# Loading, splitting and multiplying the first weight tile of an encoder kernel in pieces, and x by halves of its columns

## The reference

```python
def _rmsnorm(x, g):
    xf = x.astype(jnp.float32)
    y = xf * lax.rsqrt(jnp.mean(xf * xf, axis=-1, keepdims=True) + RMS_EPS)
    return (y * g.astype(jnp.float32)).astype(x.dtype)

def _pool_mixer(h, w_in, w_group, scale, w_out):
    b, s, _ = h.shape
    u = (h @ w_in).reshape(b, s, N_POOL_GROUPS, POOL_GROUP)
    ...
    mixed = pooled - u
    y = jnp.einsum('bsgc,gcd->bsgd', mixed, w_group).reshape(b, s, -1) * scale
    return y @ w_out

def reference(x, ...):
    for i in range(DEPTH):
        hn = _rmsnorm(x, norm_mix[i])
        ...
        x = x + y
        hn = _rmsnorm(x, norm_ffn[i])
        ...
        x = x + y
    return _rmsnorm(x, norm_final)
```

## Time and profile before

| | |
|---|---|
| median of 3 runs | 1656.31 us (1655.06 to 1656.72) |
| the profiled execution | 1656.18 us, span 1654.4 us |
| mean granted TensorE clock | 0.995 of full speed |
| TensorE busy (matmuls) | 1622.1 us, 98% |
| VectorE busy | 1205.2 us, 73% |
| ScalarE busy | 1015.3 us, 61% |
| HBM read | 455.86 MB, 276 GB/s over the span |

### The profile page before, as it was taken

The page is one execution under the profiler, slowest core; times in us unless marked ns, Lnnn a source line. Parts: engine busy times, 40 slices in busy tenths (PEclk is TensorE's granted clock), DMA queues, the critical chain, the costliest instruction groups (busy, mean ns, idle before and its releaser), DMA issues.

```text
span 1654.4 us, 22146 instructions
## 1 busy us (share of the span) xinstructions
PE 1622.1 (98%) x8139; PEld 1339.8 (81%) x8139; DVE 1205.2 (73%) x969; ACT 1015.3 (61%) x837; POOL 86.6 (5%) x107
## 2 busy tenths in 40 slices
PE   8999999999899999999999999999999999999996
PEld 6888888899699877888888888888888888888885
DVE  4554454454654568888888887887888887887886
ACT  5444443433633466767767777777777777777774
POOL 0000000050331220000000000000000000000000
PEclk9999999999999999999999999999999999999998
DMA  9555555476166417999999999999999999998992
GB/s 364 164 181 181 194 182 178 153 248 195 68 202 205 153 52 244 357 367 319 363 360 320 360 361 324 356 361 322 357 362 321 358 362 321 362 358 325 358 361 87
DMA packets 234392, 457.74 MB, mean 277 GB/s; under 512 B 9008, under 2 KB 15152, under 8 KB 234336
## 3 DMA queue, kind: packets, MB, share of 16 engines
q1 hardware_dynamic: 231216, 454.06, 78.9%
q10 hardware_dynamic: 3120, 2.91, 0.6%
HBM read 455.86 MB, written 1.08 MB: 276 GB/s over the span
## 4 chain that ended last, share of the span: by engine, by line
PE 95%; DVE 2%; ACT 1%; issue 1%; DMA 0%; SPq 0%; ACTq 0%; DVEq 0%
PE bY L273 9%; PE bY L275 9%; PE bY L274 9%; PE bG L273 8%; PE bG L274 8%; PE bG L275 8%; PE bU L275 8%; PE bU L274 8%; PE bU L273 8%; PE bS L274 3%; PE bS L275 3%; PE bS L273 3%; PE bT L493 2%; DVE logit L1155 1%; PE bX L275 1%
## 5 line engine op out<-in xcount | busy, mean ns | idle before, releaser
L263 DVE TENSOR_TENSOR wlo<-raw,whi 128x2048 fp32r<-128x2048 f32 x427 | 979.9, 2295 | 364.7 <-ACT whi L257 362.3
L257 ACT ACTIVATE whi<-raw 128x2048 fp32r<-128x2048 f32 x427 | 818.6, 1917 | 471.1 <-PE bY L275 182.2
L273 PE MATMUL bU<-whi,eTh 128*128 128x512 f32 x448 | 181.4, 405 | 0.0
L273 PE MATMUL bG<-whi,eTh 128*128 128x512 f32 x448 | 178.9, 399 | 1.1 <-ACT eTl L772 1.1
L273 PE MATMUL bY<-whi,hTh 128*128 128x512 f32 x448 | 179.0, 400 | 0.0
L274 PE MATMUL bG<-whi,eTl 128*128 128x512 f32 x448 | 178.7, 399 | 0.0
L275 PE MATMUL bG<-wlo,eTh 128*128 128x512 f32 x448 | 178.5, 398 | 0.0
L274 PE MATMUL bU<-whi,eTl 128*128 128x512 f32 x448 | 177.6, 396 | 0.0
L274 PE MATMUL bY<-whi,hTl 128*128 128x512 f32 x448 | 177.5, 396 | 0.0
L275 PE MATMUL bU<-wlo,eTh 128*128 128x512 f32 x448 | 177.5, 396 | 0.0
L275 PE MATMUL bY<-wlo,hTh 128*128 128x512 f32 x448 | 177.4, 396 | 0.0
(11 more groups left out here) (384 smaller groups left out, 2390.4 us busy)
## 6 DMA issues: line engine op xcount, KB each, us to landing
raw<-in_m_w_gate_up_dram SPq DMA_DIRECT2D x224, 1024.0 KB, 5.1
raw<-in_m_w_down_dram SPq DMA_DIRECT2D x112, 1024.0 KB, 5.0
raw<-in_b_w_in_dram SPq DMA_DIRECT2D x36, 1024.0 KB, 5.0
raw<-in_f_w_gate_up_dram SPq DMA_DIRECT2D x28, 1024.0 KB, 5.1
raw<-in_f_w_down_dram SPq DMA_DIRECT2D x14, 1024.0 KB, 4.9
raw<-in_a_w_in_dram SPq DMA_DIRECT2D x4, 1024.0 KB, 11.1
raw<-in_a_w_out_dram SPq DMA_DIRECT2D x4, 1024.0 KB, 14.0
biasrev<-toeplitz SPq DMA_DIRECT2D x32, 128.0 KB, 4.6
```

What stands on the lines that cost most here:

```text
L257: nc.scalar.activation(whi[:, t % CUT], raw[:, t % RAW], ACT.Copy).then_inc(hi_done, 1)
L263: nc.vector.tensor_tensor(wlo[:, t % CUT], raw[:, t % RAW], whi[:, t % CUT].bitcast(F32), ALU.subtract).then_inc(lo_done, 1)
L273: pe.matmul(dst, a[0], b[0], start=start, stop=False)
```

## The change

x is loaded in eight pieces instead of four, each 64 tokens by 512 columns, and has one semaphore for each half of the columns (`load_x`). The first halves go first: two from SP, two from ACT, between its loads of the identity and of `gainT`. SP then loads tile 0 in four pieces (one block of 128 rows each, `first_full`), then the second halves of x, then tile 1 and so on. ACT and DVE split tile 0 block by block (`first_hi`, `first_lo`), with 128x512 instructions instead of one of 128x2048. PE runs 16 spares, turns the first half of x, runs 6 spares, and multiplies tile 0 block by block, each into both banks as soon as its low part is there; `turn_x(0, 1)` stands behind the third block. Tile 1 is multiplied as before, behind a wait for the second half of x. `make_hi` counts the fillings of slot 0 one fewer, since tile 0 has semaphores of its own. The work in matmuls, apart from the spares, and the bytes moved are the same.

```diff
--- before.py
+++ after.py
@@ -178,7 +178,8 @@
         toep_dram = nc.dram_tensor("toeplitz", (HEADS, 512), F32, kind="Internal").ap()
 
 
-        x_in_done = sem("x_in_done")
+        x_in_done = [sem("x_in_done0"), sem("x_in_done1")]
+        first_full, first_hi, first_lo = [sem(f"first_full{b}") for b in range(4)], sem("first_hi"), sem("first_lo")
         spare_zero = sem("spare_zero")
         c_in = [sem(f"const{i}") for i in range(13)]
         raw_full = [sem(f"raw_full{i}") for i in range(RAW)]
@@ -250,8 +251,13 @@
             return ffn_tile(m_w_gate_up[0, 0], m_w_down[0, 0], t - T_MOE)
 
 
+        def load_x(engine, a, kh):
+            sl = slice(kh * 512, kh * 512 + 512)
+            engine.dma_start(x[a % 2 * 64:a % 2 * 64 + 64, a // 2, sl],
+                             x_in[0].rearrange("(m a) d -> a m d", a=4)[a][:, sl]).then_inc(x_in_done[kh], 16)
+
         def make_hi(act, t, item=0):
-            act.wait_ge(raw_full[t % RAW], item * (16 * (FFN_TILES // RAW)) + 16 * (t // RAW + 1))
+            act.wait_ge(raw_full[t % RAW], item * (16 * (FFN_TILES // RAW)) + 16 * ((t - 1) // RAW + 1))
             if t >= CUT:
                 act.wait_ge(tile_used, item * FFN_TILES + t - CUT + 1)
             nc.scalar.activation(whi[:, t % CUT], raw[:, t % RAW], ACT.Copy).then_inc(hi_done, 1)
@@ -289,9 +295,13 @@
 
         @block.sync
         def _(sp):
+            for a in range(2):
+                load_x(sp, a, 0)
+            for b in range(4):
+                sp.dma_start(raw[:, 0, b * 512:b * 512 + 512],
+                             tile_source(0)[b * P:b * P + P, :]).then_inc(first_full[b], 16)
             for a in range(4):
-                sp.dma_start(x[a % 2 * 64:a % 2 * 64 + 64, a // 2, :],
-                             x_in[0].rearrange("(m a) d -> a m d", a=4)[a]).then_inc(x_in_done, 16)
+                load_x(sp, a, 1)
 
             def load(t, item=0, src=None):
 
@@ -316,7 +326,7 @@
                     src = bass.AP(toep_dram.tensor, 2 * c * 512 + a, [[4, 64], [512, 2], [1, S]])
                     sp.dma_start(biasrev[a % 2 * 64:a % 2 * 64 + 64, c % 2, a // 2], src).then_inc(rev_full[c % 2], 16)
 
-            for t in range(T_MOE + CUT):
+            for t in range(1, T_MOE + CUT):
                 load(t)
                 for half in range(2):
                     t0 = T_ATT + half * HALF_TILES
@@ -407,7 +417,7 @@
             def turn_x(n, kh):
 
                 if n == 0:
-                    pe.wait_ge(x_in_done, 64)
+                    pe.wait_ge(x_in_done[kh], 64)
                 else:
                     pe.wait_ge(x_sum, (2, 4, 8)[n - 1] - 1 + kh)
                 for b, bank in ((0, G), (1, U)) if kh == 0 else ((2, T), (3, X)):
@@ -443,15 +453,24 @@
                     pe.matmul(S1[:], rows, cols.rearrange("p k s -> p (k s)"), start=True, stop=True)
 
             pe.wait_ge(spare_zero, 2)
-            spare(14, yTh[:, 0, 0:P], mixTh[:, 0:2])
+            spare(16, yTh[:, 0, 0:P], mixTh[:, 0:2])
             pe.wait_ge(c_in[C_IDENT], 16)
             turn_x(0, 0)
-            turn_x(0, 1)
-            spare(5, yTh[:, 0, 0:P], mixTh[:, 0:2])
-            spare(5, yTh[:, 1, P:2 * P], mixTh[:, 2:4])
-            spare(5, mixTh[:, 0, 0:P], mixTh[:, 2:4])
+            spare(6, yTh[:, 0, 0:P], mixTh[:, 0:2])
             pe.wait_ge(tx_lo, 2)
-            dense(T_IN, xTh, xTl, KH, (G, U), [lambda: pe.wait_ge(tx_lo, 4)])
+            for b in range(4):
+                pe.wait_ge(*((first_lo, b + 1) if b < 3 else (lo_done, 1)))
+                for tb, bank in enumerate((G, U)):
+                    mm = mm3(pe, bank[:], tok(xTh, xTl, b, tb), wblk(0, b), start=b == 0, stop=False)
+                if b == 2:
+                    turn_x(0, 1)
+            mm.then_inc(tile_used, 1)
+            pe.wait_ge(tx_lo, 4)
+            tile_ready(1)
+            for tb, bank in enumerate((G, U)):
+                for b in range(4):
+                    mm = mm3(pe, bank[:], tok(xTh, xTl, 4 + b, tb), wblk(1, b), start=False, stop=b == 3)
+            mm.then_inc(tile_used, 1)
 
             pe.wait_ge(c_in[C_BUCKET], 16)
             pe.wait_ge(c_in[C_RELB], 16)
@@ -774,7 +793,9 @@
             def root(n):
 
                 nc.scalar.activation(small[:, 9:10], ident[:, 0:1], ACT.Sqrt)
-                act.wait_ge(*((x_in_done, 64) if n == 0 else (x_final, 1) if n == 4 else (x_sum, (2, 4, 8)[n - 1])))
+                if n == 0:
+                    act.wait_ge(x_in_done[0], 64)
+                act.wait_ge(*((x_in_done[1], 64) if n == 0 else (x_final, 1) if n == 4 else (x_sum, (2, 4, 8)[n - 1])))
                 nc.scalar.activation((hn, squares)[n >= 3][:, 1], x[:, 1], ACT.Square, accum_out=ss[:, 1:2]).then_inc(sq_done, 1)
                 act.wait_ge(ms_done, n + 1)
                 nc.scalar.activation(std, ms, ACT.Sqrt).then_inc(std_done, 1)
@@ -793,13 +814,19 @@
                 make_hi(act, t + CUT)
 
 
-            load_const((C_IDENT, C_GAINT))
+            load_const((C_IDENT,))
+            for a in range(2, 4):
+                load_x(act, a, 0)
+            load_const((C_GAINT,))
             act.wait_ge(c_in[C_IDENT], 16)
             act.wait_ge(c_in[C_GAINT], 16)
             nc.scalar.activation(small[:, 8:9], gainT[:, 0, 0:1], ACT.Copy)
             cut_x(0, 0)
             load_const((C_BUCKET, C_RELB, C_SCALE))
-            make_hi(act, 0)
+            for b in range(4):
+                act.wait_ge(first_full[b], 16)
+                sl = slice(b * 512, b * 512 + 512)
+                nc.scalar.activation(whi[:, 0, sl], raw[:, 0, sl], ACT.Copy).then_inc(*((first_hi, 1) if b < 3 else (hi_done, 1)))
             cut_x(0, 1)
             for t in range(1, CUT):
                 make_hi(act, t)
@@ -1040,11 +1067,16 @@
 
             nc.vector.memset(yTh[:, 0:2].bitcast(F32), 0.0).then_inc(spare_zero, 1)
             cut_x(0, 0)
-            make_lo(dve, 0)
+            for b in range(4):
+                dve.wait_ge(*((first_hi, b + 1) if b < 3 else (hi_done, 1)))
+                sl = slice(b * 512, b * 512 + 512)
+                nc.vector.tensor_tensor(wlo[:, 0, sl], raw[:, 0, sl], whi[:, 0, sl].bitcast(F32),
+                                        ALU.subtract).then_inc(*((first_lo, 1) if b < 3 else (lo_done, 1)))
             cut_x(0, 1)
             for t in range(1, CUT):
                 make_lo(dve, t)
-            dve.wait_ge(x_in_done, 64)
+            dve.wait_ge(x_in_done[0], 64)
+            dve.wait_ge(x_in_done[1], 64)
             stats(0)
             for n in range(2):
                 ahead(2 * n)
```

## The result

| | before | changed |
|---|---|---|
| median | 1655.91 us (12 runs, 1654.39 to 1657.82) | 1659.25 us (12 runs, 1657.31 to 1660.53) |
| profiled execution | 1656.18 us, span 1654.4 us | 1658.49 us, span 1656.7 us |

The ratio is 1.0020, 95% interval [1.0013, 1.0028]: slower by 3.3 us, on the very line that was drawn for "can be told from no change". The interval runs from 2.2 to 4.6 us, so whether it lies beyond that line isn't settled. The forecast was 1656.6 in 1655.2 to 1659.5. The time lies inside, near the top, where the first rival stood.

The account below looks back on a forecast made before the run. TensorE, busy 98% of the span, was taken as the bound, so the opening counts by tile 1's start: 22.0 - 21.64 = +0.4 us. Added to the profiled 1656.18 us this gave 1656.6, range 1655.2 to 1659.5.

Parts of the forecast that it names:

- the first rival: TensorE's clock falls in the new gap before tile 1, costing up to 2.9 us: 1659.5 at most; chance 0.18.
- Tile 1 can start at P + 10.7: Chain through the late transposes and tile 1's split: tile 1 starts at 22.0 against 21.64 before, +0.4 us.
- P: Start of the first real matmul on TensorE; forecast 11.3 us against 15.99 before.
- It idles about 4.1 us in one piece: TensorE has no work between the end of tile 0, at 17.85, and tile 1.
- the opposite rival: The early start is kept: tile 1 follows tile 0 without a gap, 3.8 us sooner, 1652.4; chance 0.03.
- C: Moment at which ScalarE begins to read G; forecast 8.0 us, ends 7.8 and 9.82, against 9.82 before.
- Landed at 6.5 it makes ACT ready at 8.0: gainT, behind two x loads in ScalarE's queue, lands at 6.5 us; ScalarE is ready 1.5 us after it.
- C to P: From ScalarE's read of G to the first real matmul, with tile 0 split in pieces: 3.3 us.
- the 2.46 us with transposes behind it did nothing: Argument against a clock fall: TensorE's wait for x in the opening before the change left the clock up.
- rule quoted against the change: Skill's rule that idleness returns TensorE to its lower clock; applied to the new 4.1 us gap before tile 1.
- The forecast proper: Whole kernel without a clock fall: 1656.6 us, own range 1656.2 to 1657.5; chance 0.67.
- chance of 0.08: Chance that the whole kernel is slower by more than 0.2%, 3.3 us.

Follow-up runs that it names:

- after_again: The changed kernel run once more, unaltered, for a second profile; 1658.35 us.
- gain_first: The changed kernel with the load of gainT ahead of ScalarE's two loads of x; 1659.37 us, 1.0027 of before.
- filled: The changed kernel with 15 spares instead of 6 ahead of the first product and 16 between tiles 0 and 1; 1656.61 us, 1.0012 of before.
- only_turn: The kernel before with only the transposes of x's second half moved behind tile 0's third block; 1662.59 us, 1.0044 of before.
- turn_b0: The changed kernel with the transposes of x's second half behind tile 0's first block instead of the third; 1654.35 us, 0.9992 of before.
- fill: The changed kernel with 16 spare matmuls between tile 0 and tile 1; 1658.24 us, 1.0016 of before.
- early: The changed kernel with gainT ahead of ACT's loads of x, all x ahead of tile 0's pieces, second half turned before tile 0; 1653.25 us, 0.9991 of before.
- only_halves: The kernel before with x loaded in halves on two queues, tile 0 whole, second half turned before it; 1656.59 us, 1.0007 of before.
- pieces2: The kernel before with tile 0 in four pieces, x whole, three small loads issued behind the splits, 10 spares; 1652.65 us, 0.9988 of before.
- only_pieces: The kernel before with tile 0 loaded, split and multiplied in four pieces, x whole, 9 spares behind its transposes; 1651.98 us, 0.9984 of before.
- turn_filled: The kernel before with x's second half turned behind the third block, 25 spares ahead of tile 0, 16 between tiles 0 and 1; 1661.60 us, 1.0041.

## Why the prediction was right or wrong

**Right: the stall.** "Tile 1 can start at P + 10.7": 10.73 in the changed kernel, and 10.73, 10.74, 10.75 and 10.75 in `after_again`, `gain_first`, `filled` and `only_turn`. "It idles about 4.1 us in one piece": 4.04. Nothing else downstream broke: tile 2 didn't wait, the bytes were covered. The early start of 3.8 us was handed back, and the opposite rival, that it would be kept, is refuted by the same row; `turn_b0` and `only_turn` show its cause from both sides.

**Wrong in size: C.** The step "Landed at 6.5 it makes ACT ready at 8.0" failed. gainT landed at 7.50, C was 8.90. Two things lay in it. In this execution the 16 spares took 6.42 us, not 5.44, so the transposes could not start before 7.98 instead of 7.16 (the first spares run at about half pace, and how many do differs from run to run: from 4 to 6 us TensorE ran 6 of them here and 9 in `turn_b0`, where all 16 took 5.24 us; the profile gives the granted clock as 1.00 there in both, so it doesn't show this). That alone would have made C 8.64. The load of gainT, behind two loads of x, was later still and let ACT read G only at 8.90; in `fill` and `turn_b0`, where the transposes of G began at 7.30 and 6.80, it held C at 9.51 and 9.14. So the term that was mis-sized is gainT's landing, 6.5 for 7.50; C to P, 3.3, measured 3.26. The estimate counted the bytes ahead and took a share in proportion; `gain_first` (x 6.0 us from issue) against `early` (4.1 us, weights issued behind x) suggests that the weight pieces issued by SyncE delay what stands in ScalarE's queue. The Trainium skill, "DMA: Bandwidth & Descriptors", Queues, rings and completion order, has each DMA engine take turns between the queues it has work for; the two runs agree with that, without showing it directly. C's 0.9 us went one for one into tile 1: 22.89 against 22.0.

**Wrong: the chance of the clock's fall.** It was priced (up to 2.9 us; 2.2 measured from tile 1 to tile 2) and given 0.18, because "the 2.46 us with transposes behind it did nothing". One row that shows no fall was taken as evidence for a longer wait. It was the likely course: four of four profiles with 4.04 us of idle open show it, and the clock fell with shorter waits too (3.06 us in `fill`, 3.17 us in `turn_b0`, 2.04 us in `only_halves`), while it did not with the 1.77 us of the changed kernel's own first wait. The Trainium skill's rule quoted against the change ("TensorE: Matmul & The Clock Gate", Part 1: The HAM clock gate), that idle gaps are to be avoided, agrees with these profiles. The first rival's sum, 1659.5 at most, is within 0.3 us of the measured median, but by luck: C was 0.9 us too small in it and the clock 0.7 us too dear. The forecast proper, 1656.6 with no fall, missed by 2.7 us. With tile 1 late by 1.25 us and the clock by 2.2, the opening loses 3.5 us.

**The end of the account.** The first expert matmul comes 3.54 us later than before (630.37 against 626.83), but the span ended only 2.3 us later. In the profile of before the clock was low there, in the changed one it was not:

```profile
630.37 0.49 PE L279 MATMUL bG<-whi,eTh 128*128 128x512 f32 x1 [1.08 <-ACT eTl L791]
...
637.54 0.47 PE L718 MATMUL bS<-yh,selT 128*128 128x512 f32 x1 [1.31 <-DVE rank_item L1322]
```

The low clock cost bank G's matmuls 2.9 us before, but only 1.2 us of that came back. A wait of 1.3 us for rank_item, which isn't there before, took the rest: by bank U's first expert matmul the lag is 638.55 - 636.27 = 2.3 us. From the first expert matmul to the end of the span the 13 profiles take 1026.2 to 1026.3 us in ten cases, four of them with a low clock at the start of the stage, and about 1027.5 in three (before, `pieces2`, `early`). This offset is a matter of the single execution, since at the start of the expert stage the clock is low in 7 of the 13 profiles taken here and not in the others (not in either of the changed kernel); the medians, 3.3 us apart, agree with the 3.5 of the opening. So the chance of 0.08 for slower by over 0.2% was too small by the same step, the clock.

## What to carry to other kernels

Starting an engine earlier is worth only what the next tile's chain allows: follow the moved instruction on the engine that *waits* for it, with everything that is queued behind (here ScalarE waited 4.46 us for T, with tile 1's split behind it). Split a first tile in pieces, but keep what releases the second tile ahead of it, its load included. And where a change leaves TensorE idle for some microseconds in one piece, put the low clock in the sum, or fill the wait with spare matmuls, and look at every wait of the opening, not at the largest alone.

## What the runs showed of the hardware

- Waits of TensorE in the opening of 3.06, 3.17 and four times 4.04 us were each followed by a granted clock of 0.50 (1.2 GHz). Between 2 and 2.5 us both are seen: 2.04 us (`only_halves`) was followed by it, 2.10 us (`only_pieces`) and 2.11 us (`only_turn`) ahead of the transposes, 2.34 us (`only_turn` ahead of tile 0, `early` ahead of tile 1) and 2.46 us were not. The length of a wait alone doesn't decide it. With spares in both waits it stayed at 1.00 (2.4 GHz) through the opening (`filled`, `turn_filled`). The low stretch cost 1.4 (`gain_first`) to 2.7 us (`only_turn`) in tile 1.
- A small load on ScalarE's queue, 16 KB, landed 2.8 to 3.8 us after its issue with nothing but the identity ahead (seven profiles), 4.9 to 5.7 us behind two loads of x (five), and 6.7 us when SyncE had issued a whole 1 MB tile beside it as well (`only_halves`).
- From 8 to 12 us the DMAs moved 238 to 286 GB/s in the eight profiles with x loaded in halves, and 398 to 406 in the five with x whole. Why stays open: in `early` all of x had landed by 8.4 us and the rate was 272 all the same.
- Without the low clock in the expert stage 1.2 us came back of the 2.9 that it cost the first matmuls, as another wait (1.3 us) stood behind it.
